# A hybrid decoder block on eight cores: gate scans behind the next bank exit, the last value products two products later, the second gate's products two exits behind

## The reference

```python
aq, ak, av, gq, gk, gv, g_lr, g_r, gate_a, gate_b = jnp.split(proj, offs, axis=-1)
attn_o = _swa_sink_attention(aq, ak, av, attn_sinks[l])
gate_logit = (g_lr @ gla_gate_w2[l] + gla_gate_b[l]).astype(jnp.float32)
log_a = jax.nn.log_sigmoid(gate_logit) / GLA_GATE_NORMALIZER
...
    g = jnp.cumsum(chunk(log_a, GLA_DK), axis=3)
    q_dec = qc * jnp.exp(g)
    k_inv = kc * jnp.exp(-g)
...
gla_o = gla_o.reshape(B, T, GLA_HEADS * GLA_DV) * jax.nn.silu(g_r)
merged = jax.nn.sigmoid(gate_a) * attn_o + jax.nn.sigmoid(gate_b) * gla_o
h = h + merged @ w_out[l]
```

## Time and profile before

| what | value |
|---|---|
| median of three runs | 3507.01 us (3505.7 to 3509.81) |
| the profiled execution | 3509.64 us |
| its span, slowest core (core 6) | 3508.1 us; the eight cores 3502.1 to 3508.1 |
| TensorE busy | 3384.0 us, 96% |
| VectorE busy | 1983.6 us, 57% |
| ScalarE busy | 1244.6 us, 35% |
| GpSimd busy | 437.8 us, 12% |

### The profile page before, as it was taken

The page is one execution under the profiler, slowest core; times in us unless marked ns, Lnnn a source line. Parts: engine busy times, 40 slices in busy tenths (PEclk is TensorE's granted clock), DMA queues, the critical chain, the costliest instruction groups (busy, mean ns, idle before and its releaser), DMA issues.

```text
span 3508.1 us, 53846 instructions; the slowest of 8 cores (3502.1 to 3508.1 us)
## 1 busy us (share of the span) xinstructions
PE 3384.0 (96%) x18768; PEld 1784.6 (51%) x19068; DVE 1983.6 (57%) x2948; ACT 1244.6 (35%) x2423; POOL 437.8 (12%) x716
## 2 busy tenths in 40 slices
PE   7999999999999999999999999999899999999997
PEld 5565656554444444444456656565444444444443
DVE  4878787864766414673145565656547772166523
ACT  3365646564323101211125656565632210012112
POOL 1221212120100000000013131312000000000000
PEclk9999999999999999999999999999999999999998
DMA  8967776766757688776944555554847778864474
GB/s 198 219 163 175 162 170 150 178 170 179 181 121 143 107 183 173 151 142 146 227 141 127 133 135 131 139 131 124 215 132 159 161 163 181 184 117 85 80 168 132
DMA packets 183933, 541.37 MB, mean 154 GB/s; under 512 B 18929, under 2 KB 41329, under 8 KB 164721
## 3 DMA queue, kind: packets, MB, share of 16 engines
q0 software_dynamic: 77808, 304.90, 46.8%
q1 hardware_dynamic: 105858, 233.00, 20.9%
HBM read 639.28 MB, written 133.70 MB: 220 GB/s over the span
## 4 chain that ended last, share of the span: by engine, by line
PE 83%; DVE 6%; ACT 4%; issue 4%; DMA 1%; POOL 1%; DVEq 0%; ACTq 0%; POOLq 0%; SPq 0%
PE ps L1311 29%; PE ps L395 29%; PE ps L854 24%; PE ps L403 1%; PE ps L1026 1%; DMA xr_301<-x 1%; ACT fm_277 L419 1%; DVE mh L439 1%; DMA mr_73<-mtd 0%; ACT fm_267 L419 0%; ACT fm_275 L419 0%; ACT fm_269 L419 0%; ACT fm_265 L419 0%; ACT fm_271 L419 0%; DVE g_v L428 0%
## 5 line engine op out<-in xcount | busy, mean ns | idle before, releaser
L428 DVE TENSOR_TENSOR hy_0_185<-ps,hy_0_185 128x512 f32<-128x512 f32 x8 | 5.5, 692 | 224.6 <-PE ps L395 224.6
L419 ACT ACTIVATE g_Sb<-g_U,dec 128x512 bf16<-128x512 f32 x112 | 77.0, 721 | 106.3 <-DVE g_U L439 103.7
L439 DVE SCALAR_TENSOR_TENSOR mh<-ps,cols_sb,mh 128x128 bf16<-128x128 bf16 x256 | 89.2, 348 | 20.7 <-DVE mh L439 0.9
L1311 PE MATMUL ps<-v2T_142,ws_0_174 128*128 128x512 bf16 x341 | 79.0, 379 | 1.3 <-DVE m4s_125 L428 0.7
L1311 PE MATMUL ps<-v2T_203,ws_0_235 128*128 128x512 bf16 x341 | 79.0, 379 | 1.3 <-DVE m4s_125 L428 0.7
L1311 PE MATMUL ps<-v2T_142,ws_1_175 128*128 128x512 bf16 x349 | 79.1, 379 | 0.2
L1311 PE MATMUL ps<-v2T_203,ws_1_236 128*128 128x512 bf16 x349 | 79.1, 379 | 0.2
L439 DVE SCALAR_TENSOR_TENSOR g_U<-g_U,dec,ps 128x512 f32<-128x512 f32 x104 | 72.9, 742 | 2.8 <-PE ps L395 1.9
L428 DVE TENSOR_TENSOR hy_0_246<-ps,hy_0_246 128x512 f32<-128x512 f32 x4 | 2.8, 692 | 112.1 <-PE ps L395 112.1
L422 ACT COPY fb_0_237<-ps 128x512 f32<-128x512 f32 x12 | 7.0, 586 | 166.0 <-PE ps L1311 166.0
L422 ACT COPY fb_0_176<-ps 128x512 f32<-128x512 f32 x12 | 7.0, 581 | 164.6 <-PE ps L1311 164.6
(11 more groups left out here) (2090 smaller groups left out, 8889.3 us busy)
## 6 DMA issues: line engine op xcount, KB each, us to landing
wsd<-wst_74 SPq DMA_DIRECT2D x22, 512.0 KB, 2.8
wsd<-wst_75 SPq DMA_DIRECT2D x22, 512.0 KB, 2.9
wsd<-wst_76 SPq DMA_DIRECT2D x22, 512.0 KB, 6.1
wu_66<-wffn POOLq DMA_DIRECT2D x11, 1024.0 KB, 11.2
wu_68<-wffn POOLq DMA_DIRECT2D x11, 1024.0 KB, 10.8
wu_69<-wff POOLq DMA_DIRECT2D x10, 1024.0 KB, 11.4
wh_93<-wmix POOLq DMA_DIRECT2D x19, 512.0 KB, 8.9
wh_94<-wmix POOLq DMA_DIRECT2D x18, 512.0 KB, 8.9
```

Source lines behind the costliest of these rows:

```text
L419: S.op("act", lambda e: e.activation(out=o_, in_=i_, func=func, scale=scale, **kw), outs, ins)
L428: S.op("dve", lambda e: e.tensor_tensor(out=o_, in0=a, in1=b, op=op), [o_], [a, b])
L439: S.op("dve", lambda e: e.scalar_tensor_tensor(out=o_, in0=a, scalar=s, in1=b, op0=op0, op1=op1), [o_], ins)
L1311: r = e.matmul(bank[:, :], lhsT=w[:, k, :], rhs=x[:, k, :], start=first and k == 0, stop=k == 7, skip_group_check=True)
```

## The change

The scan, `dec` and the return of the work buffer become a function given to `later`. The product of the second gate goes through `later` twice. In the first chunk, heads 0 to 2, the last attention piece is due behind step 50 and not 48.

```diff
@@ st_gates
-        S.op("dve", lambda e: e.tensor_tensor_scan(out=cum[:], data0=smask[:], data1=la[0][:], initial=0.0, op0=ALU.mult,
-                                                   op1=ALU.add), [cum[:]], [smask[:], la[0][:]])
-        cl = cum[:, :].rearrange("p (a b) -> p a b", b=128)[:, :, 127]
-        act(dec[:, dk, hf * 4:hf * 4 + 4], cl, AF.Exp, scale=-1.0 / 16)
-        ffree.append(la)
+
+        def scan():
+            S.op("dve", lambda e: e.tensor_tensor_scan(out=cum[:], data0=smask[:], data1=la[0][:], initial=0.0,
+                                                       op0=ALU.mult, op1=ALU.add), [cum[:]], [smask[:], la[0][:]])
+            cl = cum[:, :].rearrange("p (a b) -> p a b", b=128)[:, :, 127]
+            act(dec[:, dk, hf * 4:hf * 4 + 4], cl, AF.Exp, scale=-1.0 / 16)
+            ffree.append(la)
+        later(scan)
@@ b_
             def times():
                 vtt(o_, two(e[1]), o_, ALU.mult)
                 ffree.append(e)
-            later(times)
+            later(lambda: later(times))
@@ due
-                due = [4, 7, 9, 12, 14, 17, 19, 22, 24, 27, 29, 31, 34] + ([43, 45, 48] if h < 3 else [42, 43, 45])
+                due = [4, 7, 9, 12, 14, 17, 19, 22, 24, 27, 29, 31, 34] + ([43, 45, 50] if h < 3 else [42, 43, 45])
```

## The result

The changed kernel took 3485.50 us, the median of three runs (3484.13 to 3488.88), against 3507.01 us for the three runs of the kernel before. The ratio is 0.9939, with an interval of 0.9917 to 0.9962: 21 us less, between 13 and 29. The forecast was 3488.0. A fourth run of each kernel (3956.08 us, with one die's cores at a granted 0.86, and 3804.56), with which the medians are 3487.19 and 3508.41, is left out here, and a **span** given in the experiments is for the same reason the median, over the dies whose four cores all had a mean granted clock of 0.989 or more, of the longest span of a die's four cores.

The account below looks back on a forecast made before the run. TensorE was taken as the bound, its idle time as what can be saved. 9.4 + 7.6 + 2x1.7 = 20.4 us, less 1.4, leaves 19.0: 3507.0 to 3488.0 us; own range 3480.5 to 3492.8, drawn out to 3498.

Parts of the forecast that it names:

- Part 1: Second chunk, scan moved behind the exit of step 10: four score-product waits for `mh` go, 9.4 us saved.
- the 0 taken for all the others: First chunk's moved scans: VectorE's queue is full, two waits of 0.49 and 1.03 us stay, 0 gained.
- ScalarE held at `dec`: Slower rival: moved scans delay `dec` and ScalarE's queue, 1.3 us at each of 22 scans, 3516.6 us; chance 0.04.
- Part 2: First chunk, heads 0 to 2: last value products after step 50 lose their waits for `a_D_141`, 3x2.52 = 7.6 us saved.
- which covers that: First chunk's head end: ScalarE's backlog nears TensorE, but the next head needs its copies only some products later.
- half clock: Behind two removed waits, one per chunk, TensorE's granted clock of 0.66 over 5 us would no longer follow.
- Part 3: Second gate's 48 `g_rs` products come one `flush` later; by itself worth 0.
- The first rival: First chunk gives its part back: ScalarE's sigmoid backlog stops TensorE at the next copies, 3495.9 us; chance 0.09.
- The price of part 3's cover: Second gate holds a work buffer one exit longer; if cover failed, 1.54 us in each of six heads, 9 us.
- the term 2x1.7: Two stretches at granted 0.66, one per chunk, (1-0.66)x5.00 = 1.70 us each, added to the saving.
- The allowance of 1.4 us: Taken off the saving: 0.2 us at seven places for small waits that come up elsewhere.
- The rival of the 0.81 clock: At first-chunk head ends, five more stretches at granted 0.81 would cost 14.4 us, giving 3502.4 us; chance 0.07.

Follow-up runs that it names:

- one scan of four: Only the scan of step 9 in the second chunk moved, four scans of the 32, against the kernel before: ratio 0.9967 (0.9954 to 0.9979).
- part 2 alone: Only the last value products moved from step 48 to step 50, against the kernel before: ratio 1.0011 (0.9992 to 1.003).
- parts 1 and 2: All scans moved and value products at step 50, second gate's products as before, against the kernel before: ratio 0.9971, span 3494.7 us.

## Why the prediction was right, and where it was not

**Part 1** came out as worked out: four waits, 9.4 us, 10.0 by spans. Exit, `mh` and scan stand in the forecast order, TensorE asks for the bank 0.7 us behind `mh` (forecast 0.6), the scan keeps its distance from its Ln. The scans of the first chunk moved nothing, the two waits of the earlier trace rows stayed, and the run with one scan of four shows that the 0 taken for all the others was right. ScalarE held at `dec`, the rival on the slow side, fell with the scans alone.

**Part 2** came out in its own rows: value products at 232.03 (forecast near 232.1) without idle, step 50 free, the exit of step 48 done at 233.04 (233.1), 3x2.52 = 7.6 us out of the entry for `a_D_141`. What failed is the step "which covers that": I took ScalarE's backlog to be covered by the next head's copies, whatever part 3 does. It isn't: with part 2 alone 4.2 to 7.7 us a core, and with parts 1 and 2 all 7.6, come back as waits for `g_am`, most of them with the half clock behind them. I followed `a_back(7)` past its neighbours on TensorE and VectorE, but not what it newly stands behind: by itself the move puts the two operations ahead of `inverse` behind a product that waits for a sigmoid. The statement that the last sigmoid ends about 1 us earlier is right for the whole change (0.8: 248.24+0.63 = 248.87, where before it released a product at 249.75) and wrong without part 3, where, counted from the product of step 48, it ends 1.5 later (24.5 us behind that product's start and not 23.0).

**Part 3** "by itself worth 0" is right and misleading. By itself it gave 1.0001; with part 2 it is worth 11 us, 3494.7 less 3483.5. The sum was right since both parts are in the change; priced one by one, the parts give half of it. The first rival ("the first chunk gives its part back") had the right mechanism, at 0.09, for the change without part 3. The price of part 3's cover, a work buffer late, didn't come up.

**The half clock** went as forecast: both stretches of 0.66 in the earlier trace rows went with the waits ahead of them, and the runs that bring waits of 1.6 to 2.5 us back bring it back behind some of them. Its size was read from one core. Behind the seven long waits the kernel before had a mix of the two levels (0.66 to 0.70 over 5 us) 23 times on its eight cores, 2 to 4 times a core, and 26 times in its second profiled execution; core 6, from which the sum takes two, is one of the two with the fewest. With 2.9 a core at 1.7 us the sum would be 21.9 (an estimate from these windows). So for the kernel, though not for this core, the term 2x1.7 was too small. The allowance of 1.4 us was too large: 0.8 of it is found, in the new wait for `g_am_116`. Both make the forecast gain smaller than the measured one, 19.0 against 20.9 and 20.5 by the spans of the table, which are medians over many dies.

**The rival of the 0.81 clock** fell: it needed more such stretches. The changed kernel's profiled execution has none on core 6 with TensorE busy 97%, and the kernel before has them in one execution and not in another. The Trainium skill ("TensorE: Matmul & The Clock Gate", section "Seeing it yourself") has 13/16 hold while the dense load lasts; by the trace, 18 us at a granted 1.00 with TensorE busy 17.95, a dense load alone doesn't bring it here. The profiled execution of before did carry two of these stretches on core 6, 2x2.9 us of its span, which the changed one lacks: so the two profiled spans differ by 24.2 us, more than the 20.4 of the sum.

## What to carry to other kernels

When work is moved past other work, write down for each engine what it newly stands *behind*, not only what it overtakes: a small operation that waits for another engine must not stand ahead of the operation that this engine needs next, or the two engines wait in a ring. Price parts of a change together where they touch the same queue; a part that is worth nothing alone can be what keeps the gain of its neighbour. And if a wait goes, look for its length under another name some 15 to 20 us later before counting it as gained. A cost that comes behind some waits only is read from all cores, not from one.

## What the runs showed of the hardware beyond what was expected

The stretches at a granted 0.81 come and go between executions of one program: 15.1 us twice on core 6 in the profiled execution of before, none there in its second one (whether the chip has a part in it was not told apart). A half-clock stretch does not follow every wait of the same length: in the profiled execution of the kernel before it followed 15 of the 24 waits of 2.5 us in the first chunk, and 8 of the 32 of 2.3 to 2.5 us in the second. And a transfer can be late by a step: the same reload of `xnT` stopped TensorE for 1.0 us on one core and for 8.6 us on another, in one execution of one program. What decides which core it hits stays open.
